# Late attention: where the probabilities of seven of eight head pairs are transposed, and which engine scales the gate sums

## The chip, the cores and the metric

The kernel runs on one core of a Trainium2 chip. The metric is the device time of one execution in microseconds (us), lower is better. Everything is float32.

## The reference, cut to what matters

Two blocks run one after the other on 256 tokens of width 1024. The change lies in the second block, which has two layers; each is an FFN, an attention mixer with two branches, and another FFN. Each branch has eight heads of width 64; the second one has only two key and value heads and a sink per head.

```
z = h @ w_in                                   # qa, ka, va, qs, ks, vs and 2048 gate columns
s = q @ k.T / sqrt(64) + bias (masked)         # per head, 256 queries x 256 keys
p = softmax(s)                                 # branch sw: the sink joins maximum and sum
o = p @ v
g = sigmoid(zg + b_gate)
merged = g[0] * (o_na @ w_branch_na) + g[1] * (o_sw @ w_branch_sw)
x = x + merged @ w_out
```

## The kernel before

The program is written by hand as one instruction list per engine, with semaphore waits between them; nothing reorders it. Each engine works strictly in its own order, and a DMA that an engine issues stands in that order too. SyncE issues the weights, one after the other, from one stream in HBM into a ring of 1 MB places, each as soon as the work on the place's last tenant has ended.

The stage of the change is the attention of each late layer (`mixer_2` for TensorE, `layer` for the others). It is a loop over eight head pairs m, four of branch na and four of sw. With each pair goes one of eight gate chunks, 256 columns of `w_in`, whose product is made by a seven-product scheme (a Strassen form): GpSimd subtracts weight blocks (`gate_weights_summed`), TensorE multiplies, VectorE adds the products to sums and scales them (`gates`, L3473), ScalarE applies the sigmoid (`gates`, L2442).

For one pair the steps are these. TensorE makes the scores (`scores`). VectorE adds the bias and finds the maximum (`softmax`, L3459), ScalarE takes the exponentials (L2459), VectorE divides by the sum (L3471). The probabilities lie with queries on the partitions, and the product with the values needs keys there. So TensorE transposes them through the identity (`turned`, eight 128x128 transposes into banks 2 and 3, the matmul at L870), ScalarE copies both banks to `y.PT` (L2467), TensorE multiplies with the values (`values`), and ScalarE copies the result to `y.OUT2` (L2471).

TensorE's order in iteration m is: `turned(m-1)`, `scores(m)`, `values(m-2)`, `gates_first(m)`, `gates_rest(m)`. `gates_first(m)` writes the banks that VectorE reads for the gate sums of m-1, and so waits for these. ScalarE's order is: the copies of `turned(m-1)`, of `values(m-2)`, the exponentials of m, `gate_first(m)` (a copy that VectorE needs for its first gate sum), the sigmoids of chunk m-1. VectorE's is: `softmax(m)`, `gates(m)`. After the loop come the last transposes and values and eight branch products.

The FFNs around this stage already transpose through DMA: VectorE transposes blocks of 32x32 in place order (L3277), ScalarE issues a DMA that writes the result to HBM (`spill`, L2313, 128 rows of 2 KB) and another that reads it back with the blocks rearranged (`bring_back`, L2322, 256 KB in 2048 pieces of 128 bytes).

## Time and profile before

| | before |
|---|---|
| median of 3 runs | 2544.48 us (2544.22 to 2552.77) |
| profiled execution, its own time | 2544.48 us |
| its span in the trace | 2543.2 us |
| TensorE busy (matmul) | 96% of the span |
| VectorE, ScalarE, GpSimd busy | 49%, 17%, 7% |
| first stage of the change (pairs 0 to 7, late layer 0) | about 1612 to 1685 us of the span |
| second stage (late layer 1) | about 2206 to 2279 us |

The span is the time from the first to the last instruction that the profile shows; 1.3 us of the execution lie around it. Issuing a DMA is not counted as busy time of an engine, though the engine's order stands still in it: such rows carry the engine's name with a q (ACTq).

### The profile page before, as it was taken

The numbers are of one execution on the slowest core, as the hardware profiler recorded it, in microseconds if no ns is written. First come the engines' busy times: TensorE is split into PE (matmuls) and PEld (weight loads), VectorE is DVE, ScalarE is ACT, GpSimd is POOL, SyncE is SP. The second block draws the span as 40 slices with busy tenths as digits, with TensorE's granted clock in tenths as the row PEclk, the third lists the DMA queues.
The fourth block names the chain that finished last, engine by engine and source line by source line (L and its number), as shares of the span: only waits on it lengthen the run. The fifth ranks groups of instructions, "written<-read, shape, count | busy, mean of one in ns | idle before, by whom it ended". The sixth has DMA issues, their size and how long they took to land.

```text
span 2543.2 us, 29763 instructions
## 1 busy us (share of the span) xinstructions
PE 2451.7 (96%) x12358; PEld 1567.5 (62%) x12358; DVE 1249.2 (49%) x2237; ACT 437.9 (17%) x1102; POOL 178.7 (7%) x126
## 2 busy tenths in 40 slices
PE   9999999888999999987889999999999999999999
PEld 5347443424578753332348866888866875888884
DVE  4994321212176621110117666545776775654774
ACT  2111110101123210000001002641101100470110
POOL 0011000000000000000000011430001003240000
PEclk9999999999999999999999999999999999999999
DMA  9854999999984499999999863415674974423671
GB/s 395 330 233 178 371 425 426 427 428 427 423 340 166 172 376 427 426 428 428 427 422 347 255 227 149 150 67 211 212 230 153 253 231 153 173 105 138 220 223 40
DMA packets 193618, 712.90 MB, mean 280 GB/s; under 512 B 117252, under 2 KB 121860, under 8 KB 128332
## 3 DMA queue, kind: packets, MB, share of 16 engines
q1 hardware_dynamic: 92304, 682.66, 67.6%
q10 hardware_dynamic: 101180, 28.35, 5.4%
q8 instruction: 98, 1.61, 0.3%
q14 instruction: 36, 0.29, 0.0%
HBM read 698.36 MB, written 12.60 MB: 280 GB/s over the span
## 4 chain that ended last, share of the span: by engine, by line
PE 79%; DMA 16%; DVE 4%; ACT 1%; issue 0%; POOL 0%; SPq 0%; another core or an unknown queue 0%; DVEq 0%; POOLq 0%
PE bank L867 77%; DMA ring<-in_stream 8%; DMA ring_high<-in_stream 4%; DMA ring_low<-in_stream 4%; PE bank L870 2%; DVE hidden L2892 1%; DVE ab_z L2717 1%; DMA hidden_turned<-normed 1%; DVE moe_results L2917 0%; POOL ab_ln_sum L3584 0%; DVE ring L3228 0%; DVE cd_y L2524 0%; DVE moe_turned L2913 0%; ACT normed L2243 0%; ACT hidden L2243 0%
## 5 line engine op out<-in xcount | busy, mean ns | idle before, releaser
L867 PE MATMUL bank<-ring,gates 128*128 128x256 f32 (+1 forms) x1760 | 433.6, 391 | 3.1 <-DVE ring L3228 2.1
L867 PE MATMUL bank<-ring,moe_chosen 128*64 128x512 f32 (+1 forms) x2352 | 400.3, 491 | 27.7 <-DMA ring<-in_stream 27.6
L867 PEld LDWEIGHTS bank<-ring,gates 128*128 128x128 f32 x1760 | 333.6, 190 | 70.7 <-issue 22.7
L867 PE MATMUL bank<-ring,normed 128*128 128x256 f32 x1448 | 339.6, 380 | 2.0 <-ACT normed L2328 1.3
L867 PEld LDWEIGHTS bank<-ring,moe_chosen 128*64 128x64 f32 x2352 | 150.6, 137 | 246.9 <-issue 200.4
L867 PEld LDWEIGHTS bank<-ring,normed 128*128 128x128 f32 x1448 | 273.1, 190 | 41.6 <-issue 3.9
L867 PE MATMUL bank<-normed,ring 128*128 128x256 f32 (+2 forms) x1152 | 289.8, 406 | 2.3 <-DVE normed L2698 1.5
L867 PEld LDWEIGHTS bank<-normed,ring 128*128 128x128 f32 x1152 | 189.4, 190 | 99.9 <-issue 85.4
L867 PE MATMUL bank<-ring,ffn_hidden 128*128 128x512 f32 (+1 forms) x416 | 179.3, 561 | 0.0
L2917 DVE COPY moe_results<-bank 32x512 f32<-32x512 f32 x36 | 24.8, 690 | 245.2 <-PE bank L867 244.8
L2908 DVE TENSOR_TENSOR moe_silu<-bank,moe_silu 128x512 f32<-128x512 f32 x32 | 22.1, 691 | 246.8 <-PE bank L867 246.8
L3228 DVE TENSOR_TENSOR ring<-ring,ring 128x1024 f32<-128x1024 f32 x117 | 142.1, 1215 | 1.6
L867 PE MATMUL bank<-ring,moe_turned 128*64 128x512 f32 x560 | 125.2, 595 | 17.4 <-DMA ring<-in_stream 14.3
L867 PEld LDWEIGHTS bank<-ring,ffn_hidden 128*128 128x128 f32 (+1 forms) x416 | 70.8, 182 | 86.3 <-issue 76.2
L2350 ACT ACTIVATE gates<-gates,small 128x256 f32<-128x256 f32 x88 | 44.4, 507 | 412.7 <-DVE gates L3241 226.2
L2164 ACT COPY moe_results<-bank 32x512 f32<-32x512 f32 x36 | 20.7, 575 | 467.1 <-PE bank L867 466.8
L867 PEld LDWEIGHTS bank<-ring,moe_turned 128*64 128x64 f32 x560 | 40.0, 137 | 98.6 <-issue 81.7
L2717 DVE SCALAR_TENSOR_TENSOR ab_z<-ab_pad_b,vectors,ab_z 128x512 f32<-128x512 f32 x120 | 90.2, 752 | 4.3
L3228 DVE TENSOR_TENSOR ring<-ring 128x1024 f32<-128x1024 f32 x71 | 85.8, 1208 | 0.0
L867 PE MATMUL bank<-ring,hidden 128*128 128x512 f32 x168 | 84.5, 592 | 0.0
L3308 DVE TENSOR_TENSOR ring<-ring 128x512 f32<-128x512 f32 x88 | 62.1, 705 | 38.2 <-PE bank L867 38.2
L3600 POOL TENSOR_TENSOR na_bias<-na_bias,na_mask 128x512 f32<-128x512 f32 x16 | 21.4, 1370 | 782.5 <-PE bank L867 782.5
(468 smaller groups left out, 2705.4 us busy)
## 6 DMA issues: line engine op xcount, KB each, us to landing
ring<-in_stream SPq DMA_DIRECT2D x318, 1024.0 KB, 7.3
ring<-in_stream SPq DMA_DIRECT2D x117, 2048.0 KB, 30.8
ring_low<-in_stream SPq DMA_DIRECT2D x7, 2048.0 KB, 43.8
ring_far<-in_stream SPq DMA_DIRECT2D x7, 2048.0 KB, 44.6
ring_high<-in_stream SPq DMA_DIRECT2D x6, 2048.0 KB, 44.8
hidden_turned<-normed ACTq DMA_DIRECT2D x44, 256.0 KB, 7.2
ffn_hidden<-hidden_turned ACTq DMA_DIRECT2D x44, 256.0 KB, 7.4
hidden<-in_stream SPq DMA_DIRECT2D x9, 1024.0 KB, 30.9
```

Source lines behind the costliest of these rows:

```text
L867: return nc.tensor.matmul(o, lhsT, rhs, start=start, stop=stop, skip_group_check=True)
L870: return nc.tensor.transpose(o, x, ident[0:x.shape[0], 0:x.shape[0]])
L2164: ins = nc.scalar.copy(m.YG[CAP * e:CAP * e + CAP, i, 0:512], bank[4][CAP * i:CAP * i + CAP, :])
L2350: nc.scalar.activation(y.sg[:, t, :], (y.C2 if t else y.C1)[:, 0, :], ACT.Silu, scale=y.rinv_t[:, t:t + 1]).then_inc(*done.up((tag, l, "si ...
L2717: ins = v.scalar_tensor_tensor(out=z_j, in0=ab.PB[:, :, k:k + T], scalar=tap("conv_b", k, j), in1=z_j, op0=ALU.mult, op1=ALU.add)
L2892: v.scalar_tensor_tensor(out=H[:, s, n, :], in0=bank[5 + n % 3][:, T * i:T * i + T], scalar=M.MOD[:, l, 5, n, s:s + 1], in1=H[:, s, n, :], ...
L2908: v.tensor_tensor(m.SG, bank[1][:, :], m.SG, ALU.mult).then_inc(*done.up((tag, "hidden", g, e)))
L2917: ins = v.tensor_copy(m.YG[CAP * e:CAP * e + CAP, i, 512:1024], bank[4][64 + CAP * i:64 + CAP * i + CAP, :])
L3228: v.tensor_tensor(tw[:, i], a, b, ALU.subtract).then_inc(*done.up((tag, l, "t", c, i)))
L3308: v.tensor_tensor(to[:, i], a, b, ALU.subtract).then_inc(*done.up((tag, l, "dt", c, i)))
L3600: nc.gpsimd.tensor_tensor(part, part, mask, ALU.add).then_inc(*done.up(("na_bias", l, t) if h == NA_H - 2 else None))
```

## The change

For pairs 0 to 6 the transposes leave TensorE. VectorE divides as before, then transposes all four tiles of the pair in one instruction of 128x1024 (blocks of 32x32), ScalarE issues four DMAs of 32 partitions that write them to HBM (`spill_probs`), and two DMAs of 256 KB that bring them back with the blocks in place (`bring_probs`, 2 times 2048 pieces of 128 bytes). Pair 7 keeps TensorE's transposes. The values run three pairs behind instead of two. The scaling of the gate sums moves from VectorE to GpSimd, behind the weight subtractions of two chunks later. VectorE does the later gate sums of m-1 at the head of iteration m. After the loop the order of values and branches is changed, and the values of pair 7 have a bank of their own.

```diff
-    y.SC = [spare[:, 512 * n:512 * n + 512].rearrange("p (t k) -> p t k", t=TT) for n in range(2)]
-    y.PT = [[x[:, 512 * n:512 * n + 512].rearrange("p (k q) -> p k q", k=TT) for n in range(2)]
-            for x in (spare[:, 1024:2048], M.ring[WEIGHT_SUMS[0]][:, SLOT:SLOT + 1024])]
+    y.SC, y.turned = spare[:, 0:1024], spare[:, 1024:2048]
+    y.pairs = [M.ring[WEIGHT_SUMS[0]][:, SLOT + 1024 * n:SLOT + 1024 * n + 1024] for n in range(2)]
+    y.PT = [[x.rearrange("p (k i q) -> p i k q", k=TT, i=2)[:, i] for i in range(2)] for x in y.pairs]
...
+def probs_of(y, m, i, t):
+
+    order = "i t k f" if m == NA_H - 1 else "k i t f"
+    return y.SC.rearrange(f"p ({order}) -> p i t k f", i=2, t=TT, f=32)[:, i, t]
...
+VALUES_AT = (6,) * (NA_H - 1) + (7,)
+LAG = 3
...
+            pe.wait_ge(*(A.at(("turned_2", l, m, 1)) if m == NA_H - 1 else S.probs_in.at((l, m))))
...
+            elif p:
+                pe.wait_ge(*A.at(("turned_2", l, NA_H - 1, n)))
...
         pairs = NA_H
         for m in range(pairs):
-            if m:
-                turned(m - 1)
             scores(m)
-            if m >= 2:
-                values(m - 2)
+            if m >= LAG:
+                values(m - LAG)
             gates_first(m)
             gates_rest(m)
             if m == 1:
                 keys_turned()
         turned(pairs - 1)
+        values(pairs - 3)
+        branch(0, 0)
+        branch(1, 0)
         values(pairs - 2)
-        branch(0, 0)
         values(pairs - 1)
-        branch(1, 0)
         branch(0, 1)
...
-            act.wait_ge(*V.at(("gate", l, c)))
+            act.wait_ge(*S.pool.at(("gate", l, c)))
...
+        def spill_probs(m):
+
+            act.wait_ge(*V.at(("turned_2", l, m)))
+            if m >= 2:
+                act.wait_ge(*S.probs_in.at((l, m - 2)))
+            for a in range(4):
+                rows = bass.AP(tensor=probs_blocks[m % 2].tensor, offset=a * 32 * 1024, ap=[[128, 32], [32 * 128, 8], [1, 128]])
+                nc.scalar.dma_start(rows, y.turned[32 * a:32 * a + 32, :].rearrange("p (k n) -> p k n", k=8)).then_inc(
+                    *S.probs_out.up((l, m) if a == 3 else None))
+
+        def bring_probs(m):
+
+            act.wait_ge(*S.probs_out.at((l, m)))
+            if m >= 2:
+                act.wait_ge(*TE.at(("values_2", l, m - 2)))
+            for k in range(TT):
+                rows = probs_blocks[m % 2].rearrange("(a k p x f) -> k p x a f", a=4, k=TT, p=P, f=32)[k]
+                to = y.pairs[m % 2].rearrange("p (k x a f) -> p k x a f", k=TT, a=4, f=32)[:, k]
+                nc.scalar.dma_start(to, rows).then_inc(*S.probs_in.up((l, m) if k == TT - 1 else None))
 
         def turned(m):
             for i in range(2):
                 act.wait_ge(*TE.at(("turned_2", l, m, i)))
-                if m >= 2:
-                    act.wait_ge(*TE.at(("values_2", l, m - 2)))
-                nc.scalar.copy(reversed_queries(flat(y.PT[m % 2][i])), bank[2 + i][:, :].rearrange("p (n q) -> p n q", q=P)).then_inc(*done.up(("turned_2", l, m, i)))
+                act.wait_ge(*TE.at(("values_2", l, m - 2)))
+                nc.scalar.copy(y.PT[m % 2][i], bank[2 + i][:, :].rearrange("p (k q) -> p k q", k=TT)).then_inc(*done.up(("turned_2", l, m, i)))
 
         def values(m):
             act.wait_ge(*TE.at(("values_2", l, m)))
-            nc.scalar.copy(y.OUT2[:, m, :], bank[6][:, 0:T]).then_inc(*done.up(("out_2", l, m)))
+            nc.scalar.copy(reversed_queries(y.OUT2[:, m, :]), bank[VALUES_AT[m]][:, 0:T].rearrange("p (n q) -> p n q", q=P)).then_inc(*done.up(("out_2", l, m)))
 
         for m in range(NA_H):
             if m:
-                turned(m - 1)
+                spill_probs(m - 1)
             if m >= 2:
-                values(m - 2)
+                bring_probs(m - 2)
             softmax(m)
+            if m >= LAG:
+                values(m - LAG)
             gate_first(m)
             if m:
                 gates(m - 1)
             if m == 1:
                 keys_out()
+        values(NA_H - 3)
         turned(NA_H - 1)
+        bring_probs(NA_H - 2)
+        gates(NA_H - 1)
         values(NA_H - 2)
-        gates(NA_H - 1)
         values(NA_H - 1)
...
+            if m:
+                dve.wait_ge(*S.probs_out.at((l, m - 1)))
+            v.transpose(y.turned, y.SC).then_inc(*done.up(("turned_2", l, m)))
...
-            by_block = y.gates_of[c].rearrange("p (n t) -> p n t", t=T)
-            v.tensor_tensor(by_block, by_block, wide(y.rinv, 2), ALU.mult).then_inc(*done.up(("gate", l, c)))
...
         for m in range(NA_H):
-            softmax(m)
+            if m:
+                gates_summed(m - 1)
+            biased(m)
+            probs(m)
+            if m < NA_H - 1:
+                turned(m)
+            gates_first(m)
             if m == 0:
                 keys_scaled()
             if m == 2:
                 keys_swapped()
-            gates(m)
+        gates_summed(NA_H - 1)
...
+    def gates_scaled(l, c):
+        pool.wait_ge(*V.at(("gate_sums", l, c)))
+        by_block = y.gates_of[c].rearrange("p (n t) -> p n t", t=T)
+        nc.gpsimd.tensor_tensor(by_block, by_block, wide(y.rinv, 2), ALU.mult).then_inc(*done.up(("gate", l, c)))
...
+            if c >= 2:
+                gates_scaled(l, c - 2)
+        for c in (KB - 2, KB - 1):
+            gates_scaled(l, c)
```

ScalarE, iteration 5 of the loop, before (`ring_53` is the weight ring's place that holds probabilities, `normed` holds OUT2):

```order
L2467 COPY hidden<-bank 128x4x128 [waits tensor_done] x2
L2471 COPY normed<-bank 128x256 [waits tensor_done]
L2455 ACT_TABLE_LOAD
L2455 ACTIVATE small<-small,sinks 128x2 [waits vector_done]
L2459 ACTIVATE hidden,small<-hidden,small 128x256 x2
L2455 ACTIVATE small<-small,sinks 128x2 [waits vector_done]
L2459 ACTIVATE hidden,small<-hidden,small 128x256 x2
L2440 COPY gates<-bank 128x128 [waits tensor_done]
L2446 ACT_TABLE_LOAD
L2446 ACTIVATE gates<-gates,layer_vectors 128x256 x2
```

The same iteration now:

```order
L2481 DMA probs_turned<-hidden 32x8x128 [waits in_probs,vector_done]
L2481 DMA probs_turned<-hidden 32x8x128 x3
L2492 DMA ring_53<-probs_turned 128x16x32 [waits out_probs]
L2492 DMA ring_53<-probs_turned 128x16x32
L2467 ACT_TABLE_LOAD
L2467 ACTIVATE small<-small,sinks 128x2 [waits vector_done]
L2471 ACTIVATE hidden,small<-hidden,small 128x8x32 x2
L2467 ACTIVATE small<-small,sinks 128x2 [waits vector_done]
L2471 ACTIVATE hidden,small<-hidden,small 128x8x32 x2
L2502 COPY normed<-bank 128x2x128 [waits tensor_done]
L2452 COPY gates<-bank 128x128 [waits tensor_done]
L2458 ACT_TABLE_LOAD
```

Six DMA issues stand where two copies stood, ahead of the exponentials; the copy of the values has gone behind them.

TensorE, from the end of one pair's gates to the end of the next pair's, before:

```order
L870 MATMUL bank2<-kept_59,hidden_56 128x128 x4
L870 MATMUL bank3<-kept_59,hidden_56 128x128 x4
L867 MATMUL bank0<-ffn_hidden_175 128x256
L867 MATMUL bank1<-ffn_hidden_175 128x256
L867 MATMUL bank0<-ffn_hidden_175 128x256
L867 MATMUL bank1<-ffn_hidden_175 128x256
L867 MATMUL bank6<-hidden_56,ffn_hidden_175 64x256 x4
L867 MATMUL bank4<-normed_57,ring3_52 128x128 x8
L867 MATMUL bank5<-gates_174,ring3_52 128x128 x4
L867 MATMUL bank4<-gates_174,ring4_53 128x128 x4
L867 MATMUL bank5<-gates_174,ring4_53 128x128 x8
L867 MATMUL bank5<-normed_57,ring4_53 128x128 x4
```

And now:

```order
L881 MATMUL bank0<-ffn_hidden_175 128x256
L881 MATMUL bank1<-ffn_hidden_175 128x256
L881 MATMUL bank0<-ffn_hidden_175 128x256
L881 MATMUL bank1<-ffn_hidden_175 128x256
L881 MATMUL bank6<-ring4_53,ffn_hidden_175 64x256 x4
L881 MATMUL bank4<-normed_57,ring3_52 128x128 x8
L881 MATMUL bank5<-gates_174,ring3_52 128x128 x4
L881 MATMUL bank4<-gates_174,ring5_54 128x128 x4
L881 MATMUL bank5<-gates_174,ring5_54 128x128 x8
L881 MATMUL bank5<-normed_57,ring5_54 128x128 x4
```

The eight transposes through the identity (`kept`) are gone from each iteration; they stand once, behind the last pair's gates.

## Rows read from the trace of the kernel before

**Rows 1.** The page, its first part: busy time of each engine.

```profile
PE 2451.7 (96%) x12358; PEld 1567.5 (62%) x12358; DVE 1249.2 (49%) x2237; ACT 437.9 (17%) x1102; POOL 178.7 (7%) x126
```

**Rows 2.** The timeline of PE: start us, us, engine, line, operation, out<-in, count.

```profile
1621.69 2.05 PE L867 MATMUL bank<-normed,ring 128*128 128x128 f32 x16
...
1640.71 2.05 PE L867 MATMUL bank<-normed,ring 128*128 128x128 f32 x16
...
1647.07 1.04 PE L870 MATMUL bank<-kept,hidden 128*128 128x128 f32 x8
1648.03 1.13 PE L867 MATMUL bank<-ffn_hidden 64*128 64x256 f32 x8
...
1650.11 2.05 PE L867 MATMUL bank<-normed,ring 128*128 128x128 f32 x16
...
1684.67 1.04 PE L870 MATMUL bank<-kept,hidden 128*128 128x128 f32 x8
```

**Rows 3.** The timeline of ACT from the end of pair 4's exponentials.

```profile
1654.27 0.24 ACT L2440 COPY gates<-bank 128x128 f32<-128x128 f32 x1
...
1657.10 1.08 ACT L2467 COPY hidden<-bank 128x512 f32<-128x512 f32 x2 [0.37 <-PE bank L870]
...
1660.02 1.28 ACT L2455 ACT_TABLE_LOAD   x1
...
1663.67 0.24 ACT L2440 COPY gates<-bank 128x128 f32<-128x128 f32 x1
```

**Rows 4.** The timeline of DVE, pair 4.

```profile
1654.79 0.61 DVE L3471 TENSOR_SCALAR hidden<-hidden,small 128x256 f32<-128x256 f32 x2
...
1656.67 0.42 DVE L3481 TENSOR_TENSOR gates<-bank,gates 128x256 f32<-128x256 f32 x1 [0.93 <-PE bank L867]
...
1657.45 0.42 DVE L3485 TENSOR_TENSOR gates<-gates,bank 128x256 f32<-128x256 f32 x1
```

**Rows 5.** The timeline of DVE, pairs 0 and 1.

```profile
1618.13 0.60 DVE L3434 TENSOR_SCALAR ffn_hidden<-bank,small 128x128 f32<-128x128 f32 x2
...
1619.38 0.41 DVE L3478 TENSOR_TENSOR ring<-bank,ring 128x256 f32<-128x256 f32 x1
...
1623.95 1.67 DVE L3471 TENSOR_SCALAR hidden<-hidden,small 128x256 f32<-128x256 f32 x2
```

**Rows 6.** What writes `normed`: durations in ns, least/median/most, first and last start.

```profile
L3277 DVE STREAM_TRANSPOSE normed<-hidden x44: 711/711/712, 1366.2 to 2473.1; 128x512 f32<-128x512 f32 x44
```

**Rows 7.** The timeline of POOL, one gate chunk: first and last of four subtractions.

```profile
1647.38 1.28 POOL L3572 TENSOR_TENSOR ring<-ring 128x512 f32<-128x512 f32 x1 [3.98 <-PE bank L867]
...
1651.53 1.26 POOL L3572 TENSOR_TENSOR ring<-ring,ring 128x512 f32<-128x512 f32 x1
```

**Rows 8.** The timeline of ACT in an FFN, DMA issues among it.

```profile
1455.27 0.59 ACTq L2322 DMA_DIRECT2D ffn_hidden<-hidden_turned  x1
...
1457.08 0.60 ACTq L2313 DMA_DIRECT2D hidden_turned<-normed  x1
...
1475.15 0.59 ACTq L2322 DMA_DIRECT2D ffn_hidden<-hidden_turned  x1
1475.96 4.81 ACTq L2313 DMA_DIRECT2D hidden_turned<-normed  x1
1480.82 0.51 ACT L2350 ACTIVATE gates<-gates,small 128x256 f32<-128x256 f32 x1 [5.36 <-issue]
```

**Rows 9.** The issue of L2313: ns it took, least/median/most.

```profile
L2313 ACTq DMA_DIRECT2D hidden_turned<-normed x44: 326/4628/16291, 1366.9 to 2473.9; - x44
```

**Rows 10.** The page, its sixth part: DMA issues, KB each, median us to landing.

```profile
ffn_hidden<-hidden_turned ACTq DMA_DIRECT2D x44, 256.0 KB, 7.4
```

**Rows 11.** Busy time by windows; last columns: granted clock, DMA share, GB/s.

```profile
1455.00:1458.00 3.00, 3.00 (x15) 2.64 (x15) 2.79 (x5) 0.77 (x2) 0.00 (x0) 1.00 0.74 176
...
1475.00:1481.00 6.00, 6.00 (x30) 5.28 (x29) 3.98 (x7) 0.56 (x2) 0.00 (x0) 1.00 0.97 353
1612.00:1685.00 73.00, 73.00 (x624) 65.38 (x623) 44.89 (x164) 55.74 (x139) 32.10 (x24) 1.00 0.34 116
```

More of the change, by code:

```diff
@@ L2498, in scalar_program @@
     turned_blocks = [nc.dram_tensor(f"hidden_turned{i}", (P * 2 * T,), F32, kind="Internal").ap() for i in range(2)]
+    probs_blocks = [nc.dram_tensor(f"probs_turned{i}", (P * 4 * T,), F32, kind="Internal").ap() for i in range(2)]
     mixer_ab()
@@ L3613, in program @@
     pool_program(nc, a, M, S, ring)
-    every = [S.tensor, S.scalar, S.vector, S.pool, S.chunk, S.distance, S.spilled, S.hidden, S.sent, *S.landed, *S.into.values()]
+    every = [S.tensor, S.scalar, S.vector, S.pool, S.chunk, S.distance, S.spilled, S.hidden, S.probs_out, S.probs_in, S.sent, *S.landed, *S.into.values()]
     return {x.name: x.table for x in every}
```

42 lines of the change are left out of this document (25 added, 17 removed).

## The prediction, made before the changed kernel ran

> **What bounds the kernel now.** I read the page's busy times first: TensorE (PE) is busy 96% of the span, no other engine above 49% [rows 1]. PE's timeline over the attention of the first late layer then shows a row of blocks without a gap. From one pair's gates to the next one's (1640.71 to 1650.11) it takes 9.40 us, and the eight transposes are 0.96 of them (1647.07 to 1648.03) [rows 2]. So PE is the bound, and the others have time to spare, though not much. ScalarE's timeline of one pair is a chain of small steps: the sigmoids behind the exponentials, two copies of 1.08 together, then a table load and exponentials, 3.65 from 1660.02 to 1663.67 [rows 3]. The last thing to read is what a DMA costs the engine that issues it, since the change puts six issues per pair on ScalarE. The FFN shows it [rows 8, 9].
>
> **What is removed.** Seven pairs in each of two layers lose 0.96 us of PE: 14 x 0.96 = 13.4 us if all else stays hidden. That is the most the change can give; 0.5% of the time, about what a measurement of this kernel can tell from no change, is 12.7 us. ScalarE loses the copies, 1.08 a pair. VectorE loses the scaling of the gate sums and gains a transpose of twice the 128x512 one's size, 2 x 0.711 = 1.42 us [rows 6].
>
> **Pair 1: a new wait on VectorE.** PE's gates of a pair wait for the gate sums of the pair before. For pair 0, VectorE has its divisions done at 1618.13, then now come the transpose (1.42), the first gate sum (0.41), the key scaling (1618.13 to 1619.38, 1.25) [rows 5], and the later sums (1656.67 to 1657.87, 1.20) [rows 4]: 1622.4, with a signal 1622.5. PE without its transposes would be there at 1621.69 - 0.96 = 1620.73 [rows 2]. So 1.8 us of a layer's 6.7 are lost at once. The gates take 9.40 - 0.96 - 2.08 (scores and values, 1648.03 to 1650.11) = 6.36, to 1628.9. ScalarE's part of the pair ends behind them with the copy of the turned keys; I allow 0.7 us (an estimate) and have it free at 1629.6.
>
> **The issues on ScalarE.** From pair 2 on, ScalarE issues four spills and two returns ahead of its exponentials. Alone, a spill issue takes 0.33 us (the least of 44) and a return issue 0.59 [rows 8, 9]: 4 x 0.33 + 2 x 0.59 = 2.5 us. But the median spill issue is 4.63 us, not 0.33. It stands right behind a return of 2048 pieces. At 1475.15 the return is issued, the next issue begins at 1475.96 and ends at 1480.77, 5.6 us behind the return's start, and the activation behind it waited 5.36 us "for issue" [rows 8]. So an issue behind a return of this kind holds the engine till most of the return's pieces are under way. The changed kernel has two such returns back to back in every pair, which the FFN never has. The hold depends on how busy the DMA engines are: 5.6 us with a DMA share of 0.97, and 2.4 us (1455.27 to 1457.68) with 0.74 [rows 8, 11]. The attention stage has 0.34 of its own [rows 11], so it is nearer to the short hold. I take 3.3 from the first return's start to the second issue's end, the second being a return too. With the four spills the block of issues, B, is 1.3 + 3.3 = 4.6 us. Its bounds: 2.5 (no hold) and 9.7 (1.3, a hold of 2.8 behind the spills' 1024 pieces, and 5.6).
>
> **One pair's chain now.** Call X the end of a pair's last exponential (1654.27 for pair 4 [rows 3]). Behind it VectorE divides till 1655.40 [rows 4], 1.1, then transposes, 1.42, and with a signal of 0.1 the spill can be issued at X + 2.6. The gate copy and the sigmoids of ScalarE are done by X + 2.5 (its next copy, at 1657.10, waited 0.37 [rows 3]), so they are hidden. Then B, then the next table load and exponentials, 3.65. The pair's period is 2.6 + B + 3.65 = 10.85 us, against 9.40 - 0.96 = 8.44 of PE. ScalarE, with the transpose ahead of it, becomes the bound. PE feels it through the gate sums, which stand behind the transpose on VectorE: they end about 4.2 us after X and PE's next gates wait there. Pairs 2 and 3 have no sinks and are a little shorter; I leave that out.
>
> **GpSimd beside VectorE.** The two divisions of a head took 0.61 us in pair 4, and 1.67 us in pair 1 [rows 4, 5], where GpSimd's subtractions ran at the same time. These begin when a pair's gates end and last 5.4 us (1647.38 to 1652.79) [rows 7]. In the slower rhythm PE's gates end about X + 4.3 + 6.36, that is 0.2 to 1.2 us before the next X, so the subtractions fall on the divisions. I add 1.05 to the four periods where such subtractions are left (pairs 2 to 5). The scaling that GpSimd takes over, one more operation of about 1.3 us beside 5.4, fits into its period and is wanted only by the sigmoids: hidden.
>
> **The sum.** X of pair 2: 1629.6 + 4.6 + 3.65 = 1637.85. Four periods of 11.9 and one of 10.85 give pair 7 at 1696.3; with division and signal, 1.2, PE's last transposes start at 1697.5 instead of 1684.67 [rows 2]: 12.8 us later. Behind them the work on PE is the same, but the values of pair 7 now stand right in front of a branch that reads them: about 0.6 us for a copy (half of one of 1.08 for two) and signals, an estimate. The last return is issued behind the copies of pair 7's transposes and has values and two branches, some 8 us, to land; one of half the size lands in 7.4 [rows 10], so I add 1 us. That is 14.4 per layer, 28.8 for both: **2573 us**. The sum is made against the profiled execution's own time, 2544.48, which is also the median of the runs; 1.3 us of it lie outside the span and don't change. Each us of B is six periods in two layers, 12 us.
>
> **Rivals.**
> *Issues stay short (no change).* If the returns leave the queue as fast as they come, B is 2.5. Then X of pair 2 is 1635.75, one period is PE's 8.44 and four are 2.6 + 2.5 + 3.65 = 8.75, the subtractions fall off the divisions as now, and the last transposes start at 1680.4, 4.3 us early. With 0.6 lost behind, 3.7 a layer are won: 2537, which is not slower. The point that decides is B at about 3.1, where six periods give the 3.7 back. For it: the light DMA load of the stage, and the hold of 2.4. Against it: 4.63 as the median. The Trainium skill (DMA: Bandwidth & Descriptors, "Issuing engines are not separate DMA queues") says that the time to start a DMA on the sequencer is usually small relative to the DMA itself; it would give this rival. The trace of before does not agree: 4.63 us of issue against 7.4 to landing.
> *Returns land late (slower still).* A spill waits for the landing of the return two pairs older, issued one iteration earlier. If both halves need 7.4 in a row, as under the FFN's load, the period is 1.3 + 14.8 = 16.1 instead of 11.9; over five periods and two layers that is 42 us more, 2615. For it: 4096 pieces a pair where the FFN has 2048 in 12 us. Against it: the stage's DMA share.
> *All hidden.* 13.4 less 3.6 for pair 1's wait and 1.2 behind the loop leaves 8.6, again 2536; a gain over 0.5% needs both waits gone.
>
> **How the numbers follow.** The forecast has 0.57 (between 2550 and 2612), short issues 0.26, late returns 0.15, and 0.02 is left for a gain past 12.7. Of the forecast's own share, 0.02 lies within 0.5% too (B under 3.3). Faster 0.02, same 0.28, slower 0.70. The range runs from 2538, just above the short issues, to 2614, which is B at 8; B at its bound of 9.7 would be 2634 and lies, like the upper half of the late returns and the lower half of the short issues, in the fifth that is left out.
>
> **What would show it.** ACTq rows for the first of the two returns short, for the second 2 to 4 us; ScalarE's exponentials starting behind them; a PE gap in front of each pair's gates from pair 3 on, released by VectorE; pairs 10.5 to 12.5 us apart; about 72,000 packets more on the queue of ScalarE. Wrong, if the second return's issue takes 0.6 us and pairs stay near 8.5 apart, or if the gaps stand before the values and end with a DMA.

## The result, and the profile after

The changed kernel takes 2588.78 us in the median of five runs (2583.85 to 2592.99). The kernel before, timed beside it on the same chip, takes 2544.29. The ratio is 1.0171, with a 95% interval of 1.0151 to 1.0191: slower by 44.5 us. The forecast was 2573, slower by 28.8, in a range of 2538 to 2614. The direction and the place were right, the size was not: 16 us are missing, and below they are looked for. B is, as in the prediction, the time of the block of six DMA issues on ScalarE.

The profiled execution took 2592.12 us (span 2590.5). TensorE's timeline gives the account by stages. I measure from the scores of pair 0 to pair 7's transposes, and on to the first product of the merged branches.

TensorE in the kernel before, layer 0, the scores of pair 0 and the merged branches (start us, us, engine, line, operation, out<-in, count):

```profile
1612.24 1.13 PE L867 MATMUL bank<-ffn_hidden 64*128 64x256 f32 x8
...
1715.59 27.79 PE L867 MATMUL bank<-hidden,ring 128*128 128x256 f32 x128
```

TensorE in the changed kernel, layer 0 (same columns, then idle before and its releaser):

```profile
1616.80 1.13 PE L881 MATMUL bank<-ffn_hidden 64*128 64x256 f32 x8
...
1647.06 1.62 PE L881 MATMUL bank<-ring,ffn_hidden 128*64 128x256 f32 x8 [4.71 <-DMA ring<-probs_turned]
1650.61 3.75 PE L881 MATMUL bank<-normed,ring 128*128 128x128 f32 x16 [1.93 <-DVE ring L3536]
1654.15 3.81 PE L881 MATMUL bank<-gates,ring 128*128 128x128 f32 x32
...
1660.87 2.05 PE L881 MATMUL bank<-normed,ring 128*128 128x128 f32 x16
...
1673.11 1.98 PE L881 MATMUL bank<-ring,ffn_hidden 128*64 128x256 f32 x8 [4.66 <-DMA ring<-probs_turned]
1676.74 3.76 PE L881 MATMUL bank<-normed,ring 128*128 128x128 f32 x16 [1.66 <-DVE gates L3536]
...
1699.76 3.75 PE L881 MATMUL bank<-normed,ring 128*128 128x128 f32 x16 [2.70 <-DVE gates L3536]
...
1708.83 1.04 PE L884 MATMUL bank<-kept,hidden 128*128 128x128 f32 x8
1709.79 1.08 PE L881 MATMUL bank<-ring,ffn_hidden 128*64 128x256 f32 x8
...
1719.47 1.08 PE L881 MATMUL bank<-ring,ffn_hidden 128*64 128x256 f32 x8 [0.47 <-ACT normed L2502]
1721.11 20.96 PE L881 MATMUL bank<-normed,ring 128*128 128x256 f32 x96 [0.56 <-ACT normed L2502]
1741.91 18.29 PE L881 MATMUL bank<-hidden,ring 128*128 128x256 f32 x84
```

The scores of pair 0 start at 1616.80, so the loop takes 92.03 us, against 72.43 before (1612.24 to 1684.67, the latter in [rows 2]). That is 19.6 more. From the last transposes to the merged product it is 33.08 against 30.92, 2.2 more. Layer 1 gives 18.8 and 2.2. Together that is 42.8 of the 47.3 us by which the two spans differ. The other 4.5 lie ahead of the stage, in work that the change doesn't touch: there the first scores start between 1610.2 and 1621.1 us in the profiles of all the kernels here.

The gapless row of blocks [rows 2] is gone. From pair 3's scores on, TensorE (PE) needs 17.6, 8.5, 18.2, 8.5 and 14.8 us from one pair to the next (the last to pair 7's transposes). In pairs 3 and 5 it stands in front of the values (4.71 and 4.66, for a return) and again in front of the gates (1.93 and 1.66, for VectorE's gate sums). In pair 7 the long wait is the one for the gate sums (2.70).

Layer 1, pairs 3 and 5, shows which of the two waits sets the pace:

```profile
2266.07 3.75 PE L881 MATMUL bank<-normed,ring 128*128 128x128 f32 x16 [5.81 <-DVE ring L3536]
...
2291.33 3.75 PE L881 MATMUL bank<-normed,ring 128*128 128x128 f32 x16 [5.28 <-DVE gates L3536]
```

There PE stands for no return in these pairs, and all the longer for the gate sums (5.81 and 5.28). The loop takes 91.25 us, hardly less. So the gate sums set the pace, and the return stands in their shadow.

The gate sums stand behind VectorE's divisions and transpose, and these behind ScalarE's exponentials. ScalarE in the changed kernel shows why they are late. These are its issues and what follows them, pairs 2 to 5 (same columns; ACTq is a DMA issue):

```profile
1636.42 4.57 ACTq L2492 DMA_DIRECT2D ring<-probs_turned  x1
1641.03 1.28 ACT L2471 ACT_TABLE_LOAD   x1 [6.96 <-DMA probs_turned<-hidden]
...
1644.31 0.24 ACT L2452 COPY ring<-bank 128x128 f32<-128x128 f32 x1
...
1648.32 1.87 ACTq L2481 DMA_DIRECT2D probs_turned<-hidden  x4
1650.23 2.03 ACTq L2492 DMA_DIRECT2D ring<-probs_turned  x2
1652.29 1.28 ACT L2471 ACT_TABLE_LOAD   x1 [5.53 <-DMA probs_turned<-hidden]
...
1658.67 2.32 ACTq L2481 DMA_DIRECT2D probs_turned<-hidden  x2
1661.03 6.19 ACTq L2492 DMA_DIRECT2D ring<-probs_turned  x2
1667.25 1.28 ACT L2467 ACT_TABLE_LOAD   x1 [8.55 <-DMA probs_turned<-hidden]
...
1675.02 1.86 ACTq L2481 DMA_DIRECT2D probs_turned<-hidden  x4
1676.91 2.00 ACTq L2492 DMA_DIRECT2D ring<-probs_turned  x2
```

The idle time in front of the table load is not a wait for data, though the profile names a DMA as its releaser. The issues stand in it: from 1648.32 to 1652.26 ScalarE does nothing but issue. In pair 2 the second return alone holds it for 4.57 us. B took 7.4, 3.9, 9.4, 3.9, 6.9 and 4.0 us for pairs 2 to 7 of layer 0; the mean over both layers is 5.7. The forecast had 4.6.

The durations of these two lines over the whole run, in ns (least/median/most; L2481 is the spills, L2492 the returns):

```profile
L2481 ACTq DMA_DIRECT2D probs_turned<-hidden x56: 309/472/1812, 1624.1 to 2314.3; - x56
L2492 ACTq DMA_DIRECT2D ring<-probs_turned x28: 587/1384/4815, 1635.8 to 2326.2; - x28
```

The least values are close to those that the FFN gave, 326 ns [rows 9] and 0.59 us [rows 8]. The most, 4.8 us, shows the hold that the forecast was about. The page of the profile lists 174,204 packets on ScalarE's queue, 73,024 more than before.

The forecast had nothing on what the last view shows. Busy time by windows in the changed kernel (columns: PE, its weight loads, VectorE, ScalarE, GpSimd, then granted clock, DMA share, GB/s):

```profile
1617.00:1709.00 92.00, 73.92 (x556) 66.12 (x555) 52.12 (x163) 47.30 (x124) 38.86 (x31) 0.87 0.64 166
1651.00:1654.00 3.00, 3.00 (x16) 3.00 (x16) 0.84 (x6) 1.70 (x2) 0.82 (x1) 0.50 0.99 168
1660.00:1663.00 3.00, 3.00 (x27) 2.47 (x26) 1.71 (x9) 0.00 (x0) 2.92 (x4) 1.00 0.82 309
1677.00:1680.00 3.00, 3.00 (x15) 3.00 (x16) 1.21 (x7) 1.05 (x1) 0.95 (x1) 0.50 0.98 190
```

Before, the stage had a granted clock of 1.00 [rows 11]. Now PE works at 0.50, that is 1.2 instead of 2.4 GHz, behind each of its long waits. The sixteen products in front of a pair's gates took 3.75 us there and 2.05 elsewhere. The gates of pairs 3, 5 and 7 took 8.18, 8.74 and 9.07 us (to 1658.79, 1685.48 and 1708.83), where pair 4 took 6.4.

### The profile page after: what moved, and what is told of

Its sections match the earlier page's. It is cut to its first block, busy times and chain, and to the rows that moved or that the text cites. A ratio compares the mean times of both kernels' runs of the same rounds, so it can differ in the third digit from the quotient of the medians.

```text
span 2590.5 us, 29613 instructions
## 1 busy us (share of the span) xinstructions
PE 2455.7 (95%) x12246; PEld 1570.9 (61%) x12246; DVE 1266.8 (49%) x2235; ACT 421.8 (16%) x1074; POOL 195.7 (8%) x142
## 3 DMA queue, kind: packets, MB, share of 16 engines
q10 hardware_dynamic: 174204, 43.03, 8.2%
## 4 chain that ended last, share of the span: by engine, by line
PE 74%; DMA 16%; DVE 5%; ACT 2%; ACTq 1%; issue 1%; POOL 0%; another core or an unknown queue 0%; SPq 0%; DVEq 0%; POOLq 0%
PE bank L881 73%; DMA ring<-in_stream 7%; DMA ring_high<-in_stream 4%; DMA ring_low<-in_stream 4%; PE bank L884 2%; DVE hidden L2928 1%; ACTq L2492 1%; DVE ab_z L2753 1%; DMA probs_turned<-hidden 1%; DMA hidden_turned<-normed 1%; ACT hidden L2471 1%; DVE hidden L3511 0%; DVE hidden L3517 0%; ACT L2467 0%; DMA vectors<-in_vectors 0%
## 5 line engine op out<-in xcount | busy, mean ns | idle before, releaser
L881 PE MATMUL bank<-normed,ring 128*128 128x256 f32 (+2 forms) x1152 | 301.5, 420 | 26.3 <-DVE gates L3536 12.3
L881 PEld LDWEIGHTS bank<-ring,normed 128*128 128x128 f32 x1448 | 274.1, 191 | 42.1 <-DMA ring<-in_stream 2.9
L881 PEld LDWEIGHTS bank<-normed,ring 128*128 128x128 f32 x1152 | 199.7, 203 | 126.0 <-issue 112.0
L881 PE MATMUL bank<-ring,ffn_hidden 128*128 128x512 f32 (+1 forms) x480 | 189.4, 545 | 13.8 <-DMA ring<-probs_turned 9.4
```

The lines of the kernel that those rows point to most:

```text
L881: return nc.tensor.matmul(o, lhsT, rhs, start=start, stop=stop, skip_group_check=True)
```

## The experiments

All ratios are to the kernel before on the same chip in the same series; its medians there lay between 2544.1 and 2545.7. Times with one value are single runs. The diffs show the lines that matter, against the changed kernel unless another is named; `...` marks lines that are left out.

### One return instead of two

The spills write the scratch in another order, so that a single DMA of 4096 pieces brings a pair back. The spills' pieces are then scattered in HBM.

```diff
-                rows = bass.AP(tensor=probs_blocks[m % 2].tensor, offset=a * 32 * 1024, ap=[[128, 32], [32 * 128, 8], [1, 128]])
...
+                rows = bass.AP(tensor=probs_blocks[m % 2].tensor, offset=a * 32 * 1024, ap=[[256, 32], [128, 2], [32 * 256, 4], [1, 128]])
...
-            for k in range(TT):
-                rows = probs_blocks[m % 2].rearrange("(a k p x f) -> k p x a f", a=4, k=TT, p=P, f=32)[k]
...
+            rows = probs_blocks[m % 2].rearrange("(a p x f) -> p x a f", a=4, p=P, f=32)
...
```

> The four spills write to HBM in another order, so that one DMA of 4096 pieces brings the pair back instead of two of 2048; bytes, pieces and waits are the same, and one issue is gone, the one that stands right behind a return. Hold theory (ScalarE stands still while it issues behind a return): the block of issues falls from a mean of 5.9 us to about 2.8, six pairs in two layers, so 35 us less than the changed kernel: about 2552 us. Landing theory (the period is set by how long the 4096 pieces take to land): no change, 2584 to 2593. VectorE theory (the gate sums behind the transpose and the divisions beside GpSimd set it): above 2580.

Measured: 2561.81 (2555.76 to 2566.88, 4 runs), ratio 1.0064 (1.0046 to 1.0083), some 27 us below the changed kernel, where 35 were expected. The durations of the single return's issue:

```profile
L2491 ACTq DMA_DIRECT2D ring<-probs_turned x14: 617/636/1137, 1632.0 to 2297.1; - x14
```

There are as many pieces in one issue, and it takes 0.64 us in the median and 1.14 at most. The second return, which stood behind another one, had taken up to 4.8. So it is the issue behind a return that is held, as the forecast said, and not the issue of many pieces as such. The scattered spills now take longer (median 636 ns), and B came to 3.7 us in the mean instead of the expected 2.8: that is the gain that is missing.

### Returns of an eighth of the pieces

```diff
-                nc.scalar.dma_start(to, rows).then_inc(*S.probs_in.up((l, m) if k == TT - 1 else None))
+                nc.scalar.dma_start(to[:, 0:1, 0:2], rows[:, 0:1, 0:2]).then_inc(*S.probs_in.up((l, m) if k == TT - 1 else None))
```

> Both returns are issued as in the changed kernel, but each brings an eighth of its pieces (256 of 2048), the rest of the probabilities stays what lay there before. Hold theory: the second issue is hardly held, the block of issues is about 3.1 us, 2550 to 2558. Landing theory: the same or a little less, 2540 to 2558. VectorE theory: above 2580, since nothing on VectorE or GpSimd has changed.

Seven eighths of the transposed probabilities are left out, so this kernel serves for its time alone.

Measured: 2558.2 (one run). B is 3.5 in the mean. With an eighth of the pieces the two returns took 1.0 to 2.3 us together instead of 2.0 to 6.2, and the time fell by 30 us, about as much as with one return. That speaks against VectorE as the cause, since nothing changed there; the hold and the landing of the returns both allowed this time.

### The scaling on GpSimd alone

The kernel before, with only the scaling moved.

```diff
-            by_block = y.gates_of[c].rearrange("p (n t) -> p n t", t=T)
-            v.tensor_tensor(by_block, by_block, wide(y.rinv, 2), ALU.mult).then_inc(*done.up(("gate", l, c)))
...
+            if c >= 2:
+                gates_scaled(l, c - 2)
```

> The kernel before with one part of the change alone: GpSimd scales the gate sums instead of VectorE, behind the subtractions of two chunks later. Hold and landing theory: the scaling is hidden, 2540 to 2549. VectorE theory (GpSimd's added work slows the divisions beside it): 2555 or more.

Measured: 2545.17 (2543.25 to 2547.21, 10 runs), ratio 0.9997 (0.9987 to 1.0007). The scaling costs and gains nothing there that can be told: it is hidden on either engine, as the forecast had it.

### The same six DMAs issued by SyncE

SyncE issues them behind the weight transfer that the end of the pair's gates sets free. ScalarE issues nothing in the loop.

```diff
+        if ring.to_be_free(i, n) in freed:
+            l, m = freed.pop(ring.to_be_free(i, n))
+            spill_probs(l, m)
+            if m:
+                bring_probs(l, m - 1)
...
-            if m:
-                spill_probs(m - 1)
-            if m >= 2:
-                bring_probs(m - 2)
             softmax(m)
```

> The same six DMAs per pair, issued by SyncE behind the weight transfer that the end of the pair's gates sets free; ScalarE issues none of them. Hold theory: ScalarE's chain of a pair is 6.3 us, under the 8.44 of TensorE, so the kernel comes out near or under the one before, 2536 to 2550. Landing theory: the pieces now queue behind the weights too, so no gain, 2584 or more. VectorE theory: above 2575.

Measured: 2553.07 (2550.03 to 2558.81, 5 runs), ratio 1.0033 (1.0020 to 1.0046). That is 36 us below the changed kernel, with the same transposes, packets and returns, and 3 above what was expected. The loop of layer 0 takes 73.35 us instead of 92.03. So ScalarE's standing still was by far the largest part. TensorE in this kernel still has these waits:

```profile
1623.93 2.02 PE L916 MATMUL bank<-normed,ring 128*128 128x128 f32 x16 [1.42 <-DVE ring L3545]
...
1641.32 1.08 PE L916 MATMUL bank<-ring,ffn_hidden 128*64 128x256 f32 x8 [1.80 <-DMA ring<-probs_turned]
1644.03 3.28 PE L916 MATMUL bank<-normed,ring 128*128 128x128 f32 x16 [1.62 <-DVE ring L3545]
...
1689.84 1.08 PE L916 MATMUL bank<-ring,ffn_hidden 128*64 128x256 f32 x8 [1.58 <-DMA ring<-probs_turned]
```

Pair 1's wait on VectorE is there, then pair 3 with a late first return, and the last return. A spill now lands in 4.7 us in the median (2.5 in the changed kernel).

### TensorE kept at work in its waits

Products of the identity into a free bank, in front of the waits of iterations 3, 5 and 7.

```diff
+            if m in (3, 5):
+                for _ in range(36):
+                    mm(bank[2][:, 0:P], ident, ident, True, True)
             if m >= LAG:
                 values(m - LAG)
+            if m in (3, 5, 7):
+                for _ in range(18 if m == 7 else 12):
+                    mm(bank[2][:, 0:P], ident, ident, True, True)
             gates_first(m)
```

> The changed kernel, with products of the identity put into TensorE's order in front of its long waits: 36 and 12 in iterations 3 and 5, 18 in iteration 7, into bank 2, which nobody reads then. They are 114 x 0.117 = 13.3 us per layer of work added in waits that hold some 17. The changed kernel had granted clock 0.50 behind these waits, and the gates of pairs 3, 5 and 7 took 8.2, 8.7 and 9.1 us instead of 6.4. Theory: the clock fell because PE had stood still, and it costs the end only where PE sets it, at pair 7 (the starts of pairs 4 and 6 are set by ScalarE's issues either way): gates back at 6.4 to 6.6 us, granted clock of the stage above 0.9, 2.7 us less per layer, 2583, 1.015 of before. Rival a: all three slow gates count in full: 6.7 us per layer less, 2575, 1.012. Rival b: the clock fell for another reason (the traffic of the DMAs): still 0.50 behind the waits, 2589 or more. Rival c: the added work itself delays PE: above 2589.

Measured: 2589.78 (4 runs), ratio 1.0178 (1.0163 to 1.0193), and a granted clock of 1.00 throughout. Rival c held: each product was two instructions, so the added work was twice what I had reckoned (8.30 us where 4.2 were meant) and took the place of the waits. The run shows that the clock stays up when PE doesn't stand still, with as much DMA traffic as in the changed kernel (share 0.65 of the stage against 0.64), so rival b fell. What the clock costs, it doesn't show. The next run has half the products:

> The run with TensorE kept at work, with 18 and 5 products of the identity in iterations 3 and 5 and 9 in iteration 7. There each product was two instructions of 0.115 us, so 36 and 12 of them took 11.2 us where the changed kernel waited about 6.6, and the added work took the place of the wait. Half of them are 4.1 + 1.2 us and 2.1 us, less than the waits. Theory (the lower clock follows PE's standing still and costs the end only at pair 7): granted clock of the stage above 0.95, gates of 6.4 to 6.6 us, 2.7 us per layer less than the changed kernel, 2583 to 2584, 1.015 of before. Rival a: all three slow gates count, 2575, 1.012. Rival b: the clock costs the end nothing, 2589, 1.017.

Measured: 2585.78 (2580.68 to 2589.06, 4 runs), ratio 1.0160 (1.0145 to 1.0175). The windows of both layers' stages:

```profile
1621.00:1708.00 87.00, 79.19 (x667) 71.64 (x667) 51.87 (x159) 44.64 (x120) 39.08 (x31) 1.00 0.69 176
2232.00:2320.00 88.00, 79.35 (x668) 71.72 (x668) 51.64 (x160) 44.80 (x121) 39.00 (x31) 1.00 0.68 176
```

The clock is 1.00 instead of 0.87, though PE still has waits of up to 1.8 us. From the first scores to the merged product a layer takes 120.6 and 121.5 us, against 125.1 and 124.3 in the changed kernel. That is 4.5 and 2.8 less. But ScalarE's blocks differ too: their sum is 3.1 us shorter in layer 0 and 0.5 longer in layer 1. Without that, the clock's own part would be 1.4 and 3.3 us, 2.4 in the mean, which is an estimate; the theory said 2.7, rival a 6.7. The total times can't settle it: 3.0 us less in the medians, and the intervals overlap. That the clock follows PE's standing still is shown; what it costs the end is not, beyond this estimate.

### The scaling back on VectorE

The changed kernel without its move to GpSimd.

```diff
+            dve.wait_ge(*done.now())
+            by_block = y.gates_of[c].rearrange("p (n t) -> p n t", t=T)
+            v.tensor_tensor(by_block, by_block, wide(y.rinv, 2), ALU.mult).then_inc(*done.up(("gate", l, c)))
```

> The changed kernel with the scaling of the gate sums back on VectorE, behind the last sum, as before the change. Theory (the issues on ScalarE set the rhythm, the scaling is covered on either engine): 1.017 of before, 2585 to 2592, the same as the changed kernel. Rival a: GpSimd's longer work slows VectorE's divisions and so the chain: the divisions of two halves back near 0.6 us in most pairs, up to 1.5 us x 5 pairs x 2 layers = 15 us less, 2574. Rival b: VectorE's extra 0.64 us per pair lies on the chain of gate sums: 14 pairs, 9 us more, 2598.

Measured: 2589.39 (2583.39 to 2595.26, 4 runs), ratio 1.0174 (1.0160 to 1.0187): the same as the changed kernel. B is 5.7 here too. With the run that moved the scaling alone, this shows that the scaling has no part in the result.

### SyncE with the first return early

As with SyncE above, and the return of pair 0 directly behind its spills, the key scaling in VectorE's wait for pair 0's exponentials (in another inner order, which the diff leaves out), the key swap behind pair 3's transpose. The first part of the diff is against the run with SyncE.

```diff
-            if m:
-                bring_probs(l, m - 1)
+            if m != 1:
+                bring_probs(l, max(m - 1, 0))
...
             biased(m)
+            if m == 0:
+                keys_scaled()
             probs(m)
             if m < NA_H - 1:
                 turned(m)
+            if m == 3:
+                keys_swapped()
             gates_first(m)
-            if m == 0:
-                keys_scaled()
-            if m == 2:
-                keys_swapped()
```

> The changed kernel with the six DMAs per pair issued by SyncE (as in the run with issues on SyncE), and three moves: the return of pair 0 directly behind its spills, the key scaling of VectorE in the wait for pair 0's exponentials instead of behind its transpose, the key swap behind pair 3's transpose instead of pair 2's first gate sum. Theory (with ScalarE free, what is left are single waits of PE: 1.42 at pair 1, 1.80 + 1.62 and about 1.6 of low clock at pair 3, 1.58 at the last return): the first three go, 1.2 + 5 us per layer, so 2553 - 12.4 = 2541, 0.998 of before; PE's pairs 8.5 apart from pair 1 to 7. Rival: the waits move on instead of going (divisions beside GpSimd, spills beside the weights' transfer): 2550 to 2553, 1.003.

Measured: 2558.42 (2554.22 to 2570.44, 6 runs), ratio 1.0056 (1.0040 to 1.0072). The theory fell, and the rival held, though the time is 5 us above what even the rival gave. Pair 1's wait went down to 0.37, and pair 3's values no longer waited, but another wait took its place. VectorE's transpose of pair 2 in this kernel:

```profile
1639.13 1.25 DVE L3526 STREAM_TRANSPOSE hidden<-hidden 128x1024 f32<-128x1024 f32 x1 [4.54 <-DMA probs_turned<-hidden]
```

It waits for the spills of pair 1, because it writes over what they read. SyncE issued these behind the early return and a weight transfer of 1 MB, and spills here took 5.3 us to land in the median. That the place of a spill in the queue decides is the theory that the next two runs try.

### Spills ahead of the weights

SyncE issues the spills of a pair, then the weight transfer, then the return of the same pair. VectorE is as in the run before. Behind the loop the values of pairs 6 and 7 come between the first two branch products.

The diff is against the run with SyncE for its order and against the changed kernel for TensorE's.

```diff
+        pair = freed.pop(ring.to_be_free(i, n), None)
+        if pair:
+            spill_probs(*pair)
         if ring.to_be_free(i, n):
...
+        if pair:
+            bring_probs(*pair)
...
         values(pairs - 3)
         branch(0, 0)
-        branch(1, 0)
         values(pairs - 2)
         values(pairs - 1)
+        branch(1, 0)
```

> As the run before it with SyncE, but SyncE issues a pair's spills ahead of the weight transfer that the pair's end sets free and its return directly behind that transfer (so a return comes one pair earlier), and behind the loop the values of pairs 6 and 7 stand between the first two branch products. Theory: spills land before the weights' pieces are queued, the returns of the last two pairs are there in time (1.6 us per layer), and the two copies of values behind the loop are covered by a branch (1.0 us, and 0.8 for one that waited): 2541 - 2 x 3.4 = 2534, 0.996 of before. Most that can be had: 13.4 us of transposes plus about 1 us, 2531. Rival: SyncE now waits for VectorE's transpose in front of the weights, so weights come later and PE waits for the ring: above 2545.

Measured: 2538.56 (2537.38 to 2540.41, 8 runs), ratio 0.9972 (0.9962 to 0.9981): faster than the changed kernel and, by 0.3%, than the one before, if 4 us short of the theory. The landing of the spills (us, least/median/most), and the waits that TensorE has left in the loop:

```profile
DMA to landing us min/median/max: 2.0/2.4/4.2
```

```profile
1621.86 2.02 PE L913 MATMUL bank<-normed,ring 128*128 128x128 f32 x16 [0.37 <-DVE ring L3542]
...
1630.43 2.02 PE L913 MATMUL bank<-normed,ring 128*128 128x128 f32 x16 [0.80 <-DVE ring L3542]
...
1645.88 1.13 PE L913 MATMUL bank<-ffn_hidden 64*128 64x256 f32 x8 [0.43 <-DVE ffn_hidden L3489]
...
1673.84 2.02 PE L913 MATMUL bank<-normed,ring 128*128 128x128 f32 x16 [0.17 <-DVE gates L3542]
```

From the first scores to the merged product it is 99.81 us in both layers, against 103.35 before: 3.5 a layer out of the 6.7 that the transposes took. That is the 7.1 us between the medians.

### The order of SyncE's DMAs alone

The same order, without the moves on VectorE and behind the loop.

> The run with issues on SyncE, with only the order of SyncE's DMAs of the fastest run so far (spills, then the weight transfer, then the return of the same pair), without its moves on VectorE and behind the loop. Theory (where a spill stands against the weights decides: landing 4.8 to 5.2 us behind them, 2.5 ahead of them, and VectorE's next transpose waits for the landing): the waits at pair 3 for the return (1.8) and the low clock behind it (1.6) and those at the last return (0.3 to 1.6) go, pair 1's 1.4 and the waits behind the loop stay: 2553 - 2 x 4.5 = 2544, 0.9995 of before. Rival: the moves on VectorE made the gain, the order little: 2550, 1.002.

Measured: 2546.15 (2542.51 to 2549.25, 11 runs), ratio 1.0005 (0.9996 to 1.0014), 7 us below the first run with SyncE and 2 above the theory. A spill lands in 2.3 us in the median. The order is worth about as much as all the other moves together, another 7.6 us. A wait of 2.21 is left at pair 3 in both layers, since the key swap stands in front of the gate sums and takes 2.24 us beside GpSimd, and 1.41 at pair 1.

### The fastest kernel with the scaling on VectorE

The scaling stands in VectorE's wait for the exponentials. The diff is against the run with spills ahead of the weights.

```diff
             biased(m)
+            if m:
+                gates_scaled(m - 1)
             if m == 0:
                 keys_scaled()
```

> The fastest run so far with the scaling of the gate sums back on VectorE, in its wait for the exponentials. Theory (GpSimd's fifth operation, 1.3 us, lengthens VectorE's second division from 0.62 to 1.43, and PE's waits of 0.80 at pair 2 and 0.43 at pair 4 come from it): second divisions back at 0.62 in most pairs, both waits gone, 1.2 us per layer less: 2536, 0.996 of before. Rival a: the divisions are no longer on a path, no change, 2538.6. Rival b: the scaling's 0.65 us stands in front of the divisions where the wait is 0.47 and so delays the transpose: 2540 to 2542.

Measured: 2536.49 (2534.53 to 2540.73, 6 runs), ratio 0.9967 (0.9955 to 0.9979). The intervals of this and the run with spills ahead overlap, so a gain over it is not shown. The waits at pairs 2 and 4 went down from 0.80 and 0.43 to 0.42 and 0.26; a new one of 0.53 (layer 1: 1.76) came at pair 6.

### The changed kernel with the weights held back

ScalarE issues as in the changed kernel. SyncE waits for a pair's spills to land before it sends the weights that the pair's end sets free.

```diff
+        if ring.to_be_free(i, n) in freed:
+            sp.wait_ge(*S.probs_out.at(freed.pop(ring.to_be_free(i, n))))
```

> The changed kernel, ScalarE issuing as there, with one wait more on SyncE: the weight transfer of 1 MB that a pair's end sets free is held till that pair's four spills have landed. In the changed kernel ScalarE's six issues took 7.4, 3.9, 9.4, 3.9, 6.9 and 4.0 us for pairs 2 to 7, long where they fell together with such a transfer. Theory (the excess over the forecast's 4.6 comes from the weights' pieces in front of theirs): all blocks near 4, pairs equally far apart instead of 8.5 and 15 to 18 in turn, six blocks x 1.9 us x 2 layers = 23 us less, 2566, 1.008 of before. Rival a: the hold comes from the return's own pieces, and only moves: blocks 5 to 6, 2580 to 2590, 1.016. Rival b: the weights then collide with the returns and land late: above 2590.

Measured: 2570.09 (2566.74 to 2570.97, 4 runs), ratio 1.0106 (1.0089 to 1.0122), 19 us below the changed kernel by one wait more, where 23 were expected. ScalarE's issues of pairs 3 to 5:

```profile
1640.85 1.87 ACTq L2484 DMA_DIRECT2D probs_turned<-hidden  x4
1642.76 2.07 ACTq L2495 DMA_DIRECT2D ring<-probs_turned  x2
...
1653.14 2.48 ACTq L2495 DMA_DIRECT2D ring<-probs_turned  x2
1661.75 1.86 ACTq L2484 DMA_DIRECT2D probs_turned<-hidden  x4
1663.65 2.12 ACTq L2495 DMA_DIRECT2D ring<-probs_turned  x2
```

Every block is now 3.9 to 5.2 us, 4.2 in the mean, so rival a, with blocks of 5 to 6 us, fell. In the changed kernel the long blocks were those beside a weight transfer, which SyncE sent there at these times (SPq is a DMA issue of SyncE):

```profile
1633.38 0.33 SPq L856 DMA_DIRECT2D ring<-in_stream  x1
...
1658.89 0.33 SPq L856 DMA_DIRECT2D ring<-in_stream  x1
...
1685.59 0.33 SPq L856 DMA_DIRECT2D ring<-in_stream  x1
```

The blocks of 7.4, 9.4 and 6.9 us began at 1633.6, 1657.8 and 1685.1. For the other three blocks the transfer was sent 4 to 8 us ahead. Layer 1 shows the same: 6.6, 7.3 and 7.0 us beside a transfer, 3.9 to 4.2 in the other three.

## Why the prediction was right or wrong

**ScalarE becomes the bound, and each us of B is 12 us: right.** Seven kernels issue on ScalarE, and B can be read from each of their traces, as the mean of twelve blocks. The prediction's line is 2573 + 12 x (B - 4.6). For the stages alone, from the first scores to the merged product in both layers, it is 28.8 + 12 x (B - 4.6) above the 206.7 us of the kernel before:

| kernel | B, us | line | median | stages, line | stages, same trace as B |
|---|---|---|---|---|---|
| short returns | 3.52 | 2560 | 2558.2 | 15.8 | 15.4 |
| one return | 3.66 | 2562 | 2561.8 | 17.6 | 18.8 |
| weights held back | 4.21 | 2568 | 2570.1 | 24.2 | 23.4 |
| kept at work, half | 5.49 | 2584 | 2585.8 | 39.5 | 35.4 |
| scaling back on VectorE | 5.67 | 2586 | 2589.4 | 41.6 | 44.1 |
| changed kernel | 5.71 | 2586 | 2588.8 | 42.1 | 42.8 |
| kept at work | 5.77 | 2587 | 2589.8 | 42.9 | 45.1 |

The line holds within 4 us of the medians, and within 4.1 us of the stages, from B = 3.5 to 5.8; a straight line through the last column rises by 12.3 us for each us of B. The rival of short issues drew its point at B = 3.1; no block here came that low with both returns whole.

**The size of B: the step that failed.** "The attention stage has 0.34 of its own [rows 11], so it is nearer to the short hold." From this B was put at 4.6; it was 5.7. In layer 0 the two returns held 2.0 to 2.1 us in the blocks without a weight transfer beside them, less than the 3.3 that were taken, and 4.9 to 6.2 us in the others. The four spills took 1.9 instead of 1.3 in the short blocks, and up to 3.2 in the long ones. The DMA share of a whole stage is a mean over stretches with a transfer and stretches with none. A pair's spills and its weight transfer are both set free near the end of its gates, so every second block met one. With the weights held back B is 4.2 and the time 2570.1. So the collision is 1.5 us of B and 19 us of time, more than the 16 that were missing. Without it the forecast would have been some 3 us too high: its 4.6 for every block had the hold too long, the spills too short and the collision not at all, and that these errors partly cancel is luck. That the long blocks are the colliding ones is shown by that run; why one comes only every second time (a long block delays the next pair until the transfer is over) is read from the times and was not tried.

**What a hold is.** The prediction read from one issue in the FFN that the engine is held till most of the return's pieces are under way. The trace of before doesn't bear this out: from the return's start at 1475.15 to the end of the held issue at 1480.77, ScalarE's queue moved 825 packets, less than half of the 2048 pieces. What ends a hold stays open; that it is longer beside a weight transfer is shown.

**What an issue costs beside its landing.** In the changed kernel a return's issue held ScalarE for 1.4 us in the median and 4.8 at most, where a return lands in 5.4 us in the median and 10.5 at most. The Trainium skill (DMA: Bandwidth & Descriptors, "Issuing engines are not separate DMA queues") says that the time to start a DMA on the sequencer is usually small relative to the DMA itself. The trace does not agree here. SyncE's weights lengthen a block of ScalarE's issues from 3.9 to 4.2 us to 6.6 to 9.4. In the same section the Trainium skill says that DMAs of all engines run on the same 16 DMA engines and interleave. The trace agrees with this.

**Smaller steps.** X is, as in the prediction, the end of a pair's last exponential. Pair 1's wait was to be 1.8 us and was 1.41. The transpose was to take 1.42 and took 1.25; the key scaling, as before, stood in front of the sums. The divisions beside GpSimd came as forecast, but in fewer pairs: the time from X to the next issue was 4.0 and 4.1 us in two periods and 2.3 to 2.5 in three, where I had 3.65 in four. That gave back 1.9 us in layer 0. With five blocks 5.2 us longer in sum (to the next table load) and exponentials 0.4 shorter, X moved from pair 2 to pair 7 in 61.36 us instead of 58.45. Ahead of that, pair 2 made 1.9 (a block 2.8 us longer, less 0.9 in smaller steps), and behind it the clock 2.0: that is the loop's 92.0 us against 85.3 of the forecast (1697.5 less 1612.24). Behind the loop I had 1.6 us and it was 2.2: 0.47 and 0.56 of waits for copies (0.6 forecast), no wait for the last return (1 forecast), and one product with values more (1.0), which the lag of three moves out of the loop. I had called the work on PE "the same" there, and missed it.

**Left out: the clock.** Nothing in the forecast was about it, since the stage ran at 1.00. The gates of pair 7 came out 2.7 us longer, and the last transposes waited for them: 3.16 us behind X instead of 1.2. The line above holds although this is left out: in layer 0 the time given back by VectorE's shorter divisions (1.9) is about as large, which is luck too.

**The rivals and the signs.** Short issues fell: the block never took 2.5. All hidden fell with it. Late returns fell as the main cause: with SyncE the same returns and packets cost 36 us less. Yet the releaser in pairs 3 and 5 of layer 0 is a return (4.71 and 4.66), and the forecast had named gaps before the values as what would make it wrong. They are there, but the wait that ends last in each of these pairs is the next one, for the gate sums, and layer 1 has that one alone (5.81 and 5.28). The sign of pairs 10.5 to 12.5 us apart failed: it holds for the mean of the five periods (61.36 / 5 = 12.3), not for two neighbouring pairs on PE, since long and short blocks take turns. In layer 0 the first return took 0.6 to 1.5 us, the second 1.4 in the short blocks and 3.8 to 4.6 in the long ones, where 2 to 4 was the sign. The packets came (73,024 more, some 72,000 forecast).

## What to carry to other kernels

The issue of one and the same return cost ScalarE 0.6 to 4.8 us here, by what stood in front of it and beside it. So look first for an engine with time to spare for a DMA of many small pieces, and put small urgent transfers ahead of the large one that the same event sets free: in SyncE's queue that order alone was worth 7 us. When a stage's DMA share is used for a hold or a landing time, read it in the stretch where the issue falls, not over the stage. And when a change opens waits in a dense stage, count the clock that TensorE loses behind them.

## What the runs showed of the hardware that I had not expected

TensorE's granted clock fell to 0.50 behind waits of 1.7 to 5.8 us, some with another just ahead of them, in a stage that was otherwise dense. In the run with the order of SyncE's DMAs alone the same wait of 2.21 us at pair 3 was followed by 1.00 in one layer and by 0.50 in the other (the sixteen products took 2.02 and 3.59 us):

```profile
1642.30:1644.10 1.80, 1.80 (x16) 1.80 (x17) 1.33 (x9) 1.25 (x5) 1.80 (x2) 1.00 1.00 378
2235.30:2238.30 3.00, 3.00 (x14) 3.00 (x15) 2.40 (x13) 2.33 (x9) 2.14 (x2) 0.50 1.01 339
```

The same kernel's eleven runs go with it: the three with a mean granted clock of 1.000 took 2542.6 to 2543.4 us, the seven with 0.995 to 0.997 took 2545.9 to 2549.3. These are means over the whole run, so they don't say where the time went.

VectorE beside GpSimd: the two divisions of a head took 0.61 us alone and 1.4 to 2.8 beside GpSimd's operations of 1.27, and the scaling, when it stood there (the fastest kernel with the scaling on VectorE), took up to 1.79 instead of 0.70. The gate sums of 256 columns, which read PSUM, took 0.42 in either case. The Trainium skill (SBUF — State Buffer, "SBUF: two separate sides") has it that VectorE, in a mode that uses two ports or with two inputs in SBUF, and GpSimd share a pair of ports as an exclusive lock: who starts first has it for the whole instruction, and the other is blocked. These times agree with that.
